# One core, two transformer layers in fp32 accuracy: the start of the recurrent stage in another order

## Chip, cores and metric

One NeuronCore of a Trainium2 chip runs the whole program in one launch. The metric is the device time in microseconds; three runs of the kernel before give a median of 2408.09 us. Its engines are called PE (matrix products; PEld is its weight load), DVE (vector), ACT (scalar), POOL (GpSimd) and SP (which here issues the DMAs).

## What is computed

Two layers on a sequence of 1024 tokens, width 1024. The first has a mixer with four branches (short convolution, stick-breaking attention, a recurrence, spatial gating), gated and merged, and a gated FFN with a short convolution; the second is an attention layer. The change lies in the recurrent branch alone. Per head (4 heads of 64) the reference is

```python
z = z + (token_shift(z) - z) * mu
...
def step(s, inp):
    r_t, w_t, k_t, v_t, a_t, b_t = inp
    sa = jnp.einsum('bhvk,bhk->bhv', s, a_t)
    s = s * w_t[:, :, None, :] + sa[..., None] * b_t[:, :, None, :] + v_t[..., None] * k_t[:, :, None, :]
    return s, jnp.einsum('bhvk,bhk->bhv', s, r_t)
```

The kernel turns the 1024 steps into 16 chunks of 64. Inside a chunk the coupling of the steps is a triangular 64x64 matrix, whose inverse is built by doubling the block size five times (five rounds); the chunks are then chained through their end states.

## The kernel before, in words

**Staging.** All projections are dense products of 128 output channels by 1024 tokens. fp32 accuracy comes from a split: POOL casts a weight block (`w_hi`, L982) and subtracts (`w_lo`, L984), and PE makes three products of it (L1276 to L1278). Block t is split by `split_weights(t)`, which waits until PE has finished block t-2, since two blocks share the buffers. Blocks 24 to 31 (`T_RW` to `T_BR` - 1) feed the recurrence; block 32 (`T_BR`) is the first of the output weights of the branches and is used only after the recurrence's rounds.

**PSUM.** There are 8 banks: `sm` is banks 0 to 3, `gp` banks 4 to 7 (slot 0 is banks 4 and 5, slot 1 banks 6 and 7). The eight dense blocks use the two slots in turn, so the last of them, block 31, ends in banks 6 and 7. ACT scales each result into `zr` (L2327), then DVE adds the shifted one, reading the same banks (`rk_shift(i)`, L2891); the semaphore `p_free0` or `p_free1` says that the slot is free.

**Preparation (DVE).** Channels come in two tiles of 128, ft = 0 and 1. After the shifts, `prep_kk`, `prep_decay`, `prep_keys` and `prep_ends` make the factors `rk_a`, `rk_b`, `rk_e`, `rk_f` and the bonus `rk_vb` of a tile. The last multiplication of `prep_keys` (L2936) makes `rk_f`. `prep_ends` multiplies the bonus (L2940, signal `rk_vb`), adds a bias to it (L2943), makes `rk_e` (L2944) and signals `rk_prep` (L2945). The order of the calls is written out by hand: ..., `prep_keys(1)`, `rk_shift(6)`, `prep_ends(1)`, `rk_shift(7)`, then the matrices.

**Matrices.** `rk_products(ft, o, lhs, rhs)` on PE (L1590) makes 64x64 products of all chunks and both heads of a tile into the bank pair o, o+1. `rk_mats_m` makes b·a into banks 2 and 3 and a·b into banks 6 and 7, `rk_mats_rest` three more: b·q into banks 0 and 1, k·q into 2 and 3, k·a into 4 and 5. DVE's `rk_mats_m` masks them: `m_t` (L2977) and `inv_t` (L2978) from banks 2 and 3, `inv` (L2980) from banks 6 and 7, then adds the identity to `inv` and `inv_t` (L2982, signals `rk_mats_taken` 1 and 2). DVE's `rk_mats_rest` (L2988) masks the other three (`rk_mats_taken` 3 to 5). PE's second pair waits for `p_free1`, that is for `rk_shift(7)`, since it writes into the banks that the shift reads.

**Rounds.** `rk_rounds(ft, beside)` has five rounds. PE multiplies the level matrix `m_lv`, which POOL makes (L1107, `rk_levels`), with `inv` (L1678), ACT copies the result (`m_p`, L2392), PE makes the next two products (L1690, L1693), and DVE adds them to `inv` and `inv_t` (L3004, L3005). Between the two halves of a round PE turns one of eight factors into token order (`rk_turn(n)`, L1626), always into banks 6 and 7. ACT copies the even turns out, DVE the odd ones: `tokens_1` (L3015), called after DVE's additions of a round; `rk_turn(n)` waits for the copy of turn n-1. So `rk_turn(2)` stands behind `tokens_1(0)`. Turns 4 to 7 belong to the second tile and read its `rk_a`, `rk_e`, `rk_f`.

After the second tile's rounds come the chain over the chunks and the merging of the branches, in which PE waits for `w_split` of block 32 for the first time.

Of the kernel before, what the change touches and what calls it, by code (L numbers as in the profile page):

```python
# [35 lines left out]
ALU = mybir.AluOpType  # L36
# [158 lines left out]
def hybrid_layers(nc, x, mix_norm_g, w_in, gate_b, sc_conv_w, sc_out, sb_out, rw_mu, rw_w0, rw_w2,  # L195
# [10 lines left out]
    with ExitStack() as ctx:  # L206
# [740 lines left out]
        def _(pool):  # L947
# [133 lines left out]
            for t in range(T_RW + 1, T_BR + 1):  # L1081
                split_weights(t)
# [29 lines left out]
            rk_levels(0)  # L1112
            pool.wait_ge(s["rk_tok_t"], 7)
# [148 lines left out]
        def _(pe):  # L1262
# [331 lines left out]
            def rk_mats_m(ft):  # L1594

                pe.wait_ge(s["rk_prep"], ft + 1)
                rk_products(ft, 2, rk_b[ft], rk_a[ft])
                if ft == 0:
                    pe.wait_ge(s["p_free1"], frees_before(P_BR))
                else:  # L1600
                    pe.wait_ge(s["rk_tok1"], 4)
                rk_products(ft, 6, rk_a[ft], rk_b[ft])

            def rk_mats_rest(ft):

                k_t, q_t = zr[:, 2 + ft, :], zr[:, ft, :]
                rk_products(ft, 0, rk_b[ft], q_t)
                pe.wait_ge(s["rk_mats_taken"], 5 * ft + 1)
                rk_products(ft, 2, k_t, q_t)
                if ft == 0:  # L1610
                    pe.wait_ge(s["p_free0"], frees_before(P_BR))
                else:
                    pe.wait_ge(s["rk_x_added"], 10)
                rk_products(ft, 4, k_t, rk_a[ft])

            def rk_turn(n):

                ft, kind = divmod(n, 4)
                if n == 0:
                    pe.wait_ge(s["rk_mats_taken"], 2)  # L1620
                else:
                    pe.wait_ge(s[f"rk_tok{(n - 1) % 2}"], (n - 1) // 2 + 1)
# [1075 lines left out]
        def _(dve):  # L2698
# [219 lines left out]

            def prep_keys(ft):
# [16 lines left out]
                wait.after(dve.tensor_tensor(chunks(f), chunks(zk), ends(ft), ALU.mult))  # L2936

            def prep_ends(ft):
                dve.wait_ge(s["rk_bonus_p"], ft + 1)
                dve.tensor_tensor(rk_vb[ft], sm[:, 2:4, :].rearrange("p a b -> p (a b)"), zr[:, 4 + ft, :], ALU.mult) \  # L2940
                    .then_inc(s["rk_vb"], 1)
                dve.wait_ge(s["rk_vb"], ft + 1)
                dve.tensor_scalar(rk_vb[ft], rk_vb[ft], pcol("gn_b", ft), None, ALU.add)  # L2943
# [18 lines left out]
            rk_shift(7)  # L2962
# [11 lines left out]
            def rk_mats_m(ft):  # L2974
# [5 lines left out]
                wait.after(dve.tensor_tensor(flat(inv), four(6), mask(9), ALU.mult))  # L2980
# [3 lines left out]
            def rk_mats_rest(ft):  # L2984
                n = 5 * ft
                for k, (dst, b, m) in enumerate(((rb_t, 0, 2), (rk_t, 2, 2), (n_t, 4, 1))):
# [30 lines left out]

            def post_xa(ft, n):
# [25 lines left out]
            rk_mats_m(0)  # L3044
            rk_mats_rest(0)
            rk_rounds(0, tokens_1)
# [465 lines left out]
```

## Time and profile before

| | us |
|---|---|
| runs: median (lowest to highest) | 2408.09 (2404.7 to 2410.54) |
| the profiled execution: its time | 2407.09 |
| its span in the trace | 2405.4 |
| PE busy in the span | 2349.3 (98%) |
| DVE, ACT, POOL busy | 1186.8, 784.9, 1129.6 |

Positions in the trace are microseconds from the span's start. In a row of the timeline the columns are start, duration, engine, line, operation, output<-inputs with sizes, count, and in brackets the idle time of the engine before it and who ended it. Rows of small instructions of one line are merged; xN is their count. A DVE instruction's successor can start about 0.1 us before its end, so the distance of two starts is less than the duration.

### The profile page before, as it was taken

Reading aid. Unit: us, or ns where it says so; the run is one execution under the profiler, and the core shown is the slowest. Engines: PE = TensorE matmul, PEld = TensorE weight load, DVE = VectorE, ACT = ScalarE, POOL = GpSimd, SP = SyncE. Lnnn points to the kernel's source line nnn. Section 1 sums busy time; section 2 is a strip of 40 time slices with the busy share of each in tenths; the row PEclk is TensorE's granted clock in tenths of the full one; section 3 lists DMA queues with packets and bytes.
Section 4 is the critical chain, followed back from the end, with each engine's and each line's share of the span. In section 5 each row is a group of like instructions: output and inputs, shape, how many; then the busy total and the mean of one; then the engine's idle time right before and its main releaser. Section 6 shows DMA issues by size and latency. Waiting matters only on the chain.

```text
span 2405.4 us, 36383 instructions
## 1 busy us (share of the span) xinstructions
PE 2349.3 (98%) x15466; PEld 1872.4 (78%) x15466; DVE 1186.8 (49%) x1460; ACT 784.9 (33%) x1217; POOL 1129.6 (47%) x771
## 2 busy tenths in 40 slices
PE   7999999999999999999999999999999999999999
PEld 6888888667778868878888887888778886666777
DVE  7811111564285364676666675333455217756621
ACT  4233331433322121254444442110433006565511
POOL 5477762333234278577777773433742220013221
PEclk9999999999999999999999999999999999999999
DMA  5233322101200056423222235222213112001024
GB/s 202 80 105 106 105 99 59 36 27 53 62 19 30 21 182 186 140 72 94 81 88 79 79 97 192 88 105 69 51 38 114 46 43 62 15 10 27 2 69 124
DMA packets 208251, 189.83 MB, mean 79 GB/s; under 512 B 16714, under 2 KB 186929, under 8 KB 207834
## 3 DMA queue, kind: packets, MB, share of 16 engines
q1 hardware_dynamic: 208090, 187.51, 24.8%
q8 instruction: 123, 2.02, 0.4%
q14 instruction: 38, 0.31, 0.0%
HBM read 141.31 MB, written 45.13 MB: 78 GB/s over the span
## 4 chain that ended last, share of the span: by engine, by line
PE 89%; DVE 6%; ACT 2%; POOL 1%; issue 1%; DMA 1%; SPq 0%; DVEq 0%; POOLq 0%; ACTq 0%
PE gp L1276 8%; PE gp L1278 8%; PE gp L1277 8%; PE sm L1839 3%; PE sm L1837 3%; PE sm L1838 3%; PE gp L1837 3%; PE gp L1839 3%; PE gp L1838 3%; PE gp L1965 3%; PE gp L1981 2%; PE gp L1422 2%; PE gp L1424 2%; PE gp L1423 2%; PE sm L1454 2%; PE gp L1454 2%
## 5 line engine op out<-in xcount | busy, mean ns | idle before, releaser
L982 POOL CAST w_hi<-w_raw 128x1024 fp32r<-128x1024 f32 (+1 forms) x97 | 107.5, 1108 | 688.3 <-PE gp L1278 317.4
L984 POOL TENSOR_TENSOR w_lo<-w_raw,w_hi 128x1024 fp32r<-128x1024 f32 (+1 forms) x105 | 284.4, 2709 | 8.3 <-ACT w_hi L2407 0.5
L1276 PE MATMUL gp<-h_hi,w_hi 128*128 128x512 f32 x656 | 260.6, 397 | 0.0
L1278 PE MATMUL gp<-h_hi,w_lo 128*128 128x512 f32 x656 | 255.5, 389 | 0.0
L1277 PE MATMUL gp<-h_lo,w_hi 128*128 128x512 f32 x656 | 255.3, 389 | 0.0
L1276 PEld LDWEIGHTS gp<-h_hi,w_hi 128*128 128x128 f32 x656 | 123.2, 188 | 29.9 <-issue 4.9
L1277 PEld LDWEIGHTS gp<-h_lo,w_hi 128*128 128x128 f32 x656 | 123.2, 188 | 27.3 <-issue 2.4
L1278 PEld LDWEIGHTS gp<-h_hi,w_lo 128*128 128x128 f32 x656 | 123.1, 188 | 25.9
L1192 POOL TENSOR_TENSOR w_lo<-w_sum,w_hi 128x512 fp32r<-128x512 f32 x66 | 96.3, 1459 | 45.7 <-ACT w_hi L2466 45.7
L2874 DVE TENSOR_TENSOR_SCAN sb_run<-sb_keep,ones_row 128x128 f32<-128x128 f32 (+7 forms) x32 | 74.1, 2355 | 84.9 <-POOL sb_keep L1030 84.9
L2631 ACT ACTIVATE att_s<-att_s,small 128x1024 f32<-128x1024 f32 (+7 forms) x128 | 98.8, 774 | 8.8 <-DVE small L3357 8.5
L1422 PE MATMUL gp<-h_hi,w_hi 128*128 128x512 f32 x208 | 86.1, 414 | 0.0
L1424 PE MATMUL gp<-h_hi,w_lo 128*128 128x512 f32 x208 | 81.6, 392 | 0.0
L2643 ACT COPY att_pt<-gp 128x512 f32<-128x512 f32 (+1 forms) x80 | 44.9, 561 | 111.2 <-PE gp L1965 110.9
L1423 PE MATMUL gp<-h_lo,w_hi 128*128 128x512 f32 x208 | 81.1, 390 | 0.0
L1965 PE MATMUL gp<-ident,att_s 128*128 128x128 f32 x576 | 77.3, 279 | 0.9 <-DVE small L3357 0.9
L2549 ACT CAST g_hi<-g_stage 128x1024 fp32r<-128x1024 f32 x22 | 23.0, 1051 | 166.2 <-DMA g_stage<-g_spill 121.3
L1837 PE MATMUL gp<-x_hi_T,w_hi 128*128 128x512 f32 x176 | 69.8, 396 | 5.9 <-DVE up_u L3195 5.2
L1142 POOL TENSOR_TENSOR merged<-merged,gated 128x1024 f32<-128x1024 f32 x24 | 64.9, 2703 | 18.1 <-DVE gated L3067 15.4
L1965 PEld LDWEIGHTS gp<-ident,att_s 128*128 128x128 f32 x576 | 61.5, 141 | 13.5 <-issue 9.3
L1861 PE MATMUL gp<-g_hi,w_hi 128*128 128x512 f32 x176 | 68.7, 390 | 2.1 <-POOL w_lo L984 1.9
L2466 ACT CAST w_hi<-w_sum 128x512 fp32r<-128x512 f32 x66 | 41.0, 621 | 90.9 <-PE gp L1839 43.6
(661 smaller groups left out, 6421.3 us busy)
## 6 DMA issues: line engine op xcount, KB each, us to landing
w_raw<-in_w_in SPq DMA_DIRECT2D x67, 512.0 KB, 4.0
gate_in<-gates_spill SPq DMA_DIRECT2D x30, 512.0 KB, 4.3
gates_spill<-gate_out SPq DMA_DIRECT2D x28, 512.0 KB, 5.9
w_raw<-in_w_up SPq DMA_DIRECT2D x22, 512.0 KB, 4.9
up_raw<-in_w_up SPq DMA_DIRECT2D x22, 512.0 KB, 5.1
g_spill<-hid SPq DMA_DIRECT2D x22, 512.0 KB, 2.6
g_stage<-g_spill SPq DMA_DIRECT2D x22, 512.0 KB, 4.4
w_raw<-in_w_down SPq DMA_DIRECT2D x22, 512.0 KB, 3.6
```

The source lines that it names most:

```text
L982: pool.tensor_copy(w_hi[:, t % 2, 0:n], w_raw[:, t % 2, 0:n]).then_inc(s["w_high"], 1)
L984: pool.tensor_tensor(w_lo[:, t % 2, 0:n], w_raw[:, t % 2, 0:n], w_hi[:, t % 2, 0:n].bitcast(F32), ALU.subtract).then_inc(s["w_split"], 1)
L1276: pe.matmul(o, wh, hi[:, k0 + k, c], start=(k == 0), stop=False)
L1277: pe.matmul(o, wh, lo[:, low[k] if low else k0 + k, c], start=False, stop=False)
L1278: mm = pe.matmul(o, wl, hi[:, k0 + k, c], start=False, stop=(k == n - 1))
L1422: pe.matmul(o, wh, h_hi[:, k, c], start=(k == 0), stop=False)
L1423: pe.matmul(o, wh, h_lo[:, k, c], start=False, stop=False)
L1424: mm = pe.matmul(o, wl, h_hi[:, k, c], start=False, stop=(k == KT - 1))
L1837: pe.matmul(o, wh, xh[:, :], start=(i < 4 and j == 0), stop=False, skip_group_check=True)
L1838: pe.matmul(o, wh, xl[:, :], start=False, stop=False, skip_group_check=True)
L1839: mm = pe.matmul(o, wl, xh[:, :], start=False, stop=(j == 3), skip_group_check=True)
L1965: mm = pe.transpose(bank(4 + r % 3)[:, P * n:P * n + P], s_buf[:, at_place(u), hh, P * k:P * k + P], ident[:, :])
```

## The change

Four edits. On PE and DVE the second product of the first tile (a·b) goes into banks 0 and 1 in place of 6 and 7, without a wait for `p_free1`, and b·q of the first tile goes into banks 6 and 7 behind that wait; the second tile keeps its banks. On DVE `rk_shift(7)` moves from ahead of the first tile's five mask operations to behind them. On DVE the second tile's `rk_f` multiplication and the rest of its `prep_ends` (bias, `rk_e`, signal `rk_prep`) become `late_ends(1)`, which runs in the first round of the first tile, after its additions and ahead of `tokens_1(0)`; in the first tile the order stays. On POOL `split_weights(T_BR)` moves from ahead of `rk_levels(0)` to behind it.

```diff
--- before.py
+++ after.py
@@ -1078,7 +1078,7 @@
                     for m, c in sb_pieces(step)[2]:
                         if c == sb_parts(m) - 1:
                             sb_cut(m)
-            for t in range(T_RW + 1, T_BR + 1):
+            for t in range(T_RW + 1, T_BR):
                 split_weights(t)
 
             def split_branch(n, y):
@@ -1110,6 +1110,7 @@
                                        ALU.mult).then_inc(s["rk_lv"], 1)
 
             rk_levels(0)
+            split_weights(T_BR)
             pool.wait_ge(s["rk_tok_t"], 7)
             for ft in range(2):
                 ends = small[:, 32 + 16 * ft:48 + 16 * ft].rearrange("p (u q) -> p q u", q=2)
@@ -1595,16 +1596,16 @@
 
                 pe.wait_ge(s["rk_prep"], ft + 1)
                 rk_products(ft, 2, rk_b[ft], rk_a[ft])
+                if ft:
+                    pe.wait_ge(s["rk_tok1"], 4)
+                rk_products(ft, 6 if ft else 0, rk_a[ft], rk_b[ft])
+
+            def rk_mats_rest(ft):
+
+                k_t, q_t = zr[:, 2 + ft, :], zr[:, ft, :]
                 if ft == 0:
                     pe.wait_ge(s["p_free1"], frees_before(P_BR))
-                else:
-                    pe.wait_ge(s["rk_tok1"], 4)
-                rk_products(ft, 6, rk_a[ft], rk_b[ft])
-
-            def rk_mats_rest(ft):
-
-                k_t, q_t = zr[:, 2 + ft, :], zr[:, ft, :]
-                rk_products(ft, 0, rk_b[ft], q_t)
+                rk_products(ft, 0 if ft else 6, rk_b[ft], q_t)
                 pe.wait_ge(s["rk_mats_taken"], 5 * ft + 1)
                 rk_products(ft, 2, k_t, q_t)
                 if ft == 0:
@@ -1617,7 +1618,7 @@
 
                 ft, kind = divmod(n, 4)
                 if n == 0:
-                    pe.wait_ge(s["rk_mats_taken"], 2)
+                    pe.wait_ge(s["rk_mats_taken"], 3)
                 else:
                     pe.wait_ge(s[f"rk_tok{(n - 1) % 2}"], (n - 1) // 2 + 1)
                 pe.wait_ge(s["rk_prep"], ft + 1)
@@ -2916,6 +2917,9 @@
                 zk = zr[:, 2 + ft, :]
                 wait.after(dve.tensor_tensor(zk, zk, rk_b[ft][:, :], ALU.mult))
 
+            def key_ends(ft):
+                wait.after(dve.tensor_tensor(chunks(rk_f[ft][:, :]), chunks(zr[:, 2 + ft, :]), ends(ft), ALU.mult))
+
             def prep_keys(ft):
                 zk, zq, e, f = zr[:, 2 + ft, :], zr[:, ft, :], rk_e[ft][:, :], rk_f[ft][:, :]
                 a, b = rk_a[ft][:, :], rk_b[ft][:, :]
@@ -2933,13 +2937,20 @@
                 dve.scalar_tensor_tensor(a, rk_kk[:, :], -1.0, rk_lx[:, :], ALU.mult, ALU.mult)
                 dve.tensor_tensor(zq, zq, rk_l[:, :], ALU.mult)
                 wait.after(dve.tensor_copy(decay_end(ft), rk_l[:, C - 1:T:C]))
-                wait.after(dve.tensor_tensor(chunks(f), chunks(zk), ends(ft), ALU.mult))
+                if ft == 0:
+                    key_ends(0)
 
             def prep_ends(ft):
                 dve.wait_ge(s["rk_bonus_p"], ft + 1)
                 dve.tensor_tensor(rk_vb[ft], sm[:, 2:4, :].rearrange("p a b -> p (a b)"), zr[:, 4 + ft, :], ALU.mult) \
                     .then_inc(s["rk_vb"], 1)
+                if ft == 0:
+                    late_ends(0)
+
+            def late_ends(ft):
                 dve.wait_ge(s["rk_vb"], ft + 1)
+                if ft:
+                    key_ends(ft)
                 dve.tensor_scalar(rk_vb[ft], rk_vb[ft], pcol("gn_b", ft), None, ALU.add)
                 wait.after(dve.tensor_tensor(chunks(rk_e[ft][:, :]), chunks(rk_b[ft][:, :]), ends(ft), ALU.mult))
                 dve.tensor_copy(small[:, 80:81], ones[:, 0:1]).then_inc(s["rk_prep"], 1)
@@ -2959,7 +2970,6 @@
             prep_keys(1)
             rk_shift(6)
             prep_ends(1)
-            rk_shift(7)
 
             def flat(x):
                 return x[:, :, :, :].rearrange("p h u c -> p (h u) c")
@@ -2977,13 +2987,13 @@
                 dve.tensor_tensor(flat(m_t), four(2), mask(1), ALU.mult).then_inc(s["rk_m"], 1)
                 dve.tensor_tensor(flat(inv_t[ft]), four(2), mask(3), ALU.mult)
                 dve.wait_ge(s["rk_mats"], n + 2)
-                wait.after(dve.tensor_tensor(flat(inv), four(6), mask(9), ALU.mult))
+                wait.after(dve.tensor_tensor(flat(inv), four(6 if ft else 0), mask(9), ALU.mult))
                 for x in (inv, inv_t[ft]):
                     dve.tensor_tensor(flat(x), flat(x), mask(0), ALU.add).then_inc(s["rk_mats_taken"], 1)
 
             def rk_mats_rest(ft):
                 n = 5 * ft
-                for k, (dst, b, m) in enumerate(((rb_t, 0, 2), (rk_t, 2, 2), (n_t, 4, 1))):
+                for k, (dst, b, m) in enumerate(((rb_t, 0 if ft else 6, 2), (rk_t, 2, 2), (n_t, 4, 1))):
                     dve.wait_ge(s["rk_mats"], n + 3 + k)
                     dve.tensor_tensor(flat(dst[ft]), four(b), mask(m), ALU.mult).then_inc(s["rk_mats_taken"], 1)
 
@@ -3015,6 +3025,12 @@
                 dve.tensor_copy((a_tok, b_tok, k_tok, v_tok)[kind][ft][:, :, :],
                                 gp[:, 1, :].rearrange("p (u c) -> p u c", u=NB)).then_inc(s["rk_tok1"], 1)
 
+            def beside_0(n):
+
+                if n == 0:
+                    late_ends(1)
+                tokens_1(n)
+
             def post_xa(ft, n):
                 dve.wait_ge(s["rk_post"], n)
                 dve.tensor_copy(flat(xa[ft]), chunks(gp[:, 1, :])).then_inc(s["rk_post1"], 1)
@@ -3042,8 +3058,9 @@
 
             dve.wait_ge(s["masks"], 1)
             rk_mats_m(0)
+            rk_shift(7)
             rk_mats_rest(0)
-            rk_rounds(0, tokens_1)
+            rk_rounds(0, beside_0)
             rk_mats_rest(1)
             rk_rounds(1, post_1)
             post_xa(1, 7)
```

## Rows read from the trace of the kernel before

**Rows 1.** The page: part 1, first engines, and part 4, the chain by engine.
```profile
PE 2349.3 (98%) x15466; PEld 1872.4 (78%) x15466; DVE 1186.8 (49%) x1460; ACT 784.9 (33%) x1217; POOL 1129.6 (47%) x771
...
PE 89%; DVE 6%; ACT 2%; POOL 1%; issue 1%; DMA 1%; SPq 0%; DVEq 0%; POOLq 0%; ACTq 0%
```

**Rows 2.** Timeline, 690 to 730 us: DVE's preparation and masks, ACT's last dense block.
```profile
700.41 1.23 DVE L2936 TENSOR_TENSOR rk_f<-zr,small 128x1024 f32<-128x1024 f32 x1
...
704.25 0.76 DVE L2943 TENSOR_SCALAR rk_lx<-rk_lx,col 128x1024 f32<-128x1024 f32 x1
...
704.63 1.12 ACT L2327 ACTIVATE zr<-gp,small 128x1024 f32<-128x1024 f32 x1 [12.87 <-PE gp L1278]
...
706.24 1.27 DVE L2891 SCALAR_TENSOR_TENSOR zr<-gp,col,zr 128x1023 f32<-128x1023 f32 x1
...
707.55 1.22 DVE L2977 TENSOR_TENSOR m_t<-sm,masks 128x1024 f32<-128x1024 f32 x1
...
711.07 1.23 DVE L2982 TENSOR_TENSOR inv<-inv,masks 128x1024 f32<-128x1024 f32 x1
...
712.21 1.22 DVE L2982 TENSOR_TENSOR inv_t<-inv_t,masks 128x1024 f32<-128x1024 f32 x1
...
713.35 1.22 DVE L2988 TENSOR_TENSOR rb_t<-sm,masks 128x1024 f32<-128x1024 f32 x1
```

**Rows 3.** The same timeline: PE's five matrix products and the first round.
```profile
704.53 1.16 PE L1590 MATMUL sm<-rk_a,rk_b 64*64 64x64 f32 x64
...
707.57 1.16 PE L1590 MATMUL gp<-rk_b,rk_a 64*64 64x64 f32 x64 [1.88 <-DVE zr L2891]
...
708.55 1.11 PE L1590 MATMUL sm<-zr,rk_b 64*64 64x64 f32 x64
...
712.35 1.72 PE L1590 MATMUL sm<-zr 64*64 64x64 f32 x64 [2.69 <-DVE inv L2982]
...
713.82 1.95 PE L1590 MATMUL gp<-rk_a,zr 64*64 64x64 f32 x64
...
715.53 2.33 PE L1678 MATMUL sm<-inv,m_lv 64*64 64x64 f32 x64
```

**Rows 4.** Busy time by window: window, length, engines, granted clock, DMA share, GB/s.
```profile
712.30:713.80 1.50, 1.45 (x64) 1.45 (x68) 1.50 (x2) 0.00 (x0) 0.00 (x0) 0.64 0.00 0
...
713.80:715.50 1.70, 1.70 (x76) 1.70 (x70) 1.70 (x2) 0.00 (x0) 0.00 (x0) 0.50 0.05 10
...
715.50:717.80 2.30, 2.30 (x77) 2.23 (x69) 1.42 (x2) 0.59 (x1) 0.80 (x1) 0.86 0.00 0
...
717.80:719.00 1.20, 1.20 (x16) 1.03 (x16) 0.00 (x0) 0.67 (x2) 1.20 (x1) 1.00 0.07 14
```

**Rows 5.** Timeline, 722 to 732 us: second round of the first tile.
```profile
723.71 2.08 PE L1678 MATMUL sm<-inv,m_lv 64*64 64x64 f32 x64
...
724.01 1.22 DVE L3015 COPY b_tok<-gp 128x1024 f32<-128x1024 f32 x1
...
725.72 1.09 PE L1626 MATMUL gp<-ident,rk_f 128*128 128x128 f32 x8
...
725.88 2.37 POOL L1107 TENSOR_TENSOR m_lv<-m_t,masks 128x1024 f32<-128x1024 f32 x1 [4.20 <-PE sm L1678]
```

**Rows 6.** Timeline, 690 to 698 us: DVE and POOL beside each other.
```profile
690.75 1.72 POOL L982 CAST w_hi<-w_raw 128x1024 fp32r<-128x1024 f32 x1 [8.25 <-PE gp L1278]
...
691.49 2.06 DVE L2928 TENSOR_TENSOR rk_b<-rk_kk,rk_a 128x1024 f32<-128x1024 f32 x1
...
692.55 3.25 POOL L984 TENSOR_TENSOR w_lo<-w_raw,w_hi 128x1024 fp32r<-128x1024 f32 x1
...
693.58 3.30 DVE L2931 TENSOR_TENSOR rk_b<-rk_b,rk_f 128x1024 f32<-128x1024 f32 x1
```

**Rows 7.** Timeline of POOL, 690 to 800 us.
```profile
708.85 2.36 POOL L1107 TENSOR_TENSOR m_lv<-m_t,masks 128x1024 f32<-128x1024 f32 x1 [13.05 <-DVE m_t L2977]
...
742.77 4.07 POOL L1117 TENSOR_TENSOR s_step<-masks,small 128x512 f32<-128x512 f32 x4 [6.59 <-PE gp L1626]
```

## Prediction

> **What bounds the kernel now.** I read the page first: PE is busy for 98% of the span and holds 89% of the chain that ended last [rows 1]. So a change of order can only give back time in which PE stands idle or slow, and can cost any time in which it makes PE stand idle. I then read the timeline where the diff works, 690 to 730 us, engine by engine. PE runs its last dense block without a gap and makes the first 64x64 product at 704.53 [rows 3]. Then it stops twice: 1.88 us until the last shift on DVE is done, and 2.69 us until DVE has masked `inv` [rows 3]. DVE in the same stretch never stops: `rk_f` at 700.41, bias at 704.25, last shift at 706.24, `m_t` at 707.55, and the five mask operations to 713.35 [rows 2]. So here the chain is DVE's, and after 712.35 it is PE's again. Third, the granted clock by window: after the second stop it is 0.64 and then 0.50 of full, that is 1.2 GHz in place of 2.4, and it is back at 1.00 by 717.8 [rows 4]. From 717.8 on the first tile's rounds are bound by PE, with DVE waiting.
>
> **Working: up to the first round.** The start of PE's first product stays at 704.53, since PE is full until then. It ends at 705.69 [rows 3], and DVE, now free, starts `m_t` at about 705.8 in place of 707.55: 1.75 us won. `inv` reads banks 0 and 1, whose product PE makes at once, one product of 0.98 us later (708.55 less 707.57 [rows 3]), well before DVE asks. The five operations take 713.35 - 707.55 = 5.80 us [rows 2], to 711.60. Only then comes the last shift, 1.27 us [rows 2], to 712.87. Its other input, ACT's scaling, is done at 705.75 [rows 2] and holds nothing. PE's b·q product waits for this shift, and k·q and k·a stand behind it in PE's order. PE answered 0.06 us after the shift in the kernel before (707.57 against 707.51 [rows 2, 3]), so it restarts at 712.93, against 712.35 before: the shift and the addition to `inv_t` now stand ahead of it and eat the 1.75 us. And it then owes three products before the rounds, where it owed two.
>
> The two took 3.18 us (712.35 to 715.53). At 1.2 GHz one costs 715.53 - 713.82 = 1.71 us, at 2.4 GHz 0.98 us [rows 3, 4]. PE will have stood still from about 706.7 to 712.93, 6.2 us, longer than the stop after which the clock fell here, so I take a fall. With two products slow and one fast I get 4.40 us, and the rounds start at 717.33 in place of 715.53. The first round's product then runs at full clock, 2.08 in place of 2.33 us [rows 3, 5], which returns 0.25. Sum: **+1.55 us**. Bounds: all three fast gives 715.87 and +0.1; all three slow, and the next one too, gives 718.06 and +2.5.
>
> **Working: the first round.** `late_ends(1)` holds the `rk_f` multiplication, 1.23 us, and bias, `rk_e` and signal, 706.24 - 704.25 = 1.99 us [rows 2]: 3.2 us. Queued behind it on DVE is `tokens_1(0)`, which started at 724.01 and lasts 1.22 us [rows 5]; behind that copy waits `rk_turn(2)` on PE, since the turns share one pair of banks, and behind the turn all the rest of PE's second round. On the old time scale the copy would run from 727.2 to 728.45, and PE would turn at 728.5 in place of 725.72 [rows 5]: **+2.8 us**. DVE's idle time in a round does not cover this, because the work stands ahead of the copy.
>
> It can be more. POOL makes a level matrix at 725.88 for 2.37 us [rows 5], reading two SBUF operands. In the new order `rk_e`, a DVE multiplication of SBUF operands, would be asked for at about 724.01 + 1.23 + 0.76 = 726.0, less up to 0.1 for the overlap of successive DVE instructions [rows 2, 5], just behind POOL's request, while the bias operation still runs. What such a meeting costs is to be seen in rows 6: POOL's cast ends at 692.47, and the DVE multiplication asked for at 691.49 ends at 693.55, 1.08 us after it; the subtraction ends at 695.80, and the multiplication asked for at 693.58 ends at 696.88, again 1.08 us after it. So DVE waits out the whole POOL instruction. Here POOL would run from about 726.0 to 728.4, `rk_e` end at 729.45, the copy at 730.65, and PE turn at 730.7: +5.0 us in place of +2.8. Ends: 2.8 and 5.0. I take **+5.0**, because in rows 6 the one who asked first went first each time.
>
> A row can be held against this: `inv`'s addition at 711.07 took 1.23 us beside a level matrix that ran from 708.85 to 711.21 [rows 2, 7]. Only 0.14 us of them overlap, so it decides little. The Trainium skill (SBUF — State Buffer, section "SBUF: two separate sides") calls the pair an exclusive lock, which a vector operation with two SBUF inputs and a GpSimd operation that reads SBUF take from each other for a whole instruction; by it this term would be 5.0, by the bare durations 2.8.
>
> **Working: the clock again.** PE would stand from about 725.8 to 730.7, 4.9 us. Before, the clock fell after a stop of 2.69 us and the slow stretch cost 0.49 + 0.73 + 0.25 = 1.5 us against full-clock durations [rows 3, 5]. Ends: 0 and 1.5, as the clock stayed up after the stop of 1.88 [rows 3] and fell after the longer one. The stop ahead is nearer to the longer: **+1.5**.
>
> **What costs nothing.** The split of block 32 leaves 690.75 to 695.80. DVE gets back 2.06 + 3.30 less twice 1.22, 2.9 us [rows 2, 6], and with the 3.2 us of late ends is ready long before 704.5; but PE is full until then, so this wins nothing beyond the 1.75 already counted. Should that cover be gone, it would be worth up to that much again. The split's new place is POOL's idle time before 742.77, 6.59 us [rows 7]; even at the durations with DVE in the way, 1.72 + 3.25 [rows 6], it fits. Without that gap the diagonal steps would be late, which nobody asks for until the second tile's rounds. DVE's work there reads PSUM. SP's next weight load waits for this split, but stands behind a wait for a product of the second tile's rounds. ACT's sigmoid of the gate input and its table load wait for the last shift and move to about 713 to 715.5, ahead of its first copy of the round. The second tile's `rk_prep` is needed only at turn 4.
>
> **Sum.** 1.55 + 5.0 + 1.5 = 8.05, say +8.1 us. Behind the stage PE's work is the same and shifts whole. Against the profiled execution (span 2405.4, time 2407.09) this is 2415.2; the median of the runs is 1.0 above that execution, so I forecast **2416.2**. A measurement of this kernel tells some 0.2%, 4.8 us, from no change.
>
> **Rivals.**
> - *POOL comes second.* `rk_e` gets ahead of the level matrix, less than 0.1 us decides [rows 5]. 1.55 + 2.8 is +4.4, with the clock's second fall +5.9: 2412.5 to 2414.0. For it: the margin. Against it: rows 6.
> - *Not slower.* The clock stays at 2.4 GHz through both stops. Then the first part costs 0.1 only, and with POOL second the whole is 0.1 + 2.8 = +2.9: 2411.0, inside 0.2%. Place: PE's restarts at 712.9 and in the second round; it decides if both windows show 1.00. For it: the stop of 1.88 us left the clock up. Against it: both new stops are longer than 2.69.
> - *Worse.* Clock down for all three products and once more as long in the second round: 2.5 + 5.0 + 3.0 = +10.5, 2418.6.
> - *Faster.* The turn does not feel the late ends, or the first shift and mask order turns out shorter than I add up: then 1.75 us of earlier `m_t` and 1.5 us of a fall that goes away are the most there is, 2404.8 to 2408. The code speaks against it, since the wait for the copy is written out.
>
> **Chances.** Forecast 0.45, POOL second 0.25, not slower 0.14, worse 0.10, faster 0.06. POOL second lies on both sides of 4.8 us, half and half. So slower 0.68, within 0.2% 0.26, faster 0.06. The range goes from 2410 (one us under the not-slower case, for the measurement) to 2419 (the worse case): it leaves out the faster case and little of the others.
>
> **What would show it.** In the profile after: `m_t` near 705.8; the last shift near 711.6; PE idle some 6 us, ended by L2891, with a granted clock of 0.5 behind it; the first L1678 near 717.3; in the second round L1626 with an idle time of 2.7 (POOL second) or 4.9 us (POOL first), ended by L3015, and `rk_e` at 1.2 or near 3.4 us. I am wrong if the first L1678 comes at 715.5 or sooner, if L1626 has no such idle time, or if something behind 860 us takes the shift up.

## The result, and the profile after

| | kernel before | changed kernel |
|---|---|---|
| median (lowest to highest), us | 2409.32 (2404.7 to 2410.7) | 2419.57 (2417.55 to 2421.22) |
| ratio, 95% interval | | 1.0047 (1.0035 to 1.0059) |
| span of the profiled execution | 2405.4 | 2416.3 |
| mean granted clock of PE in it | 0.996 | 0.992 |

The changed kernel is slower: the medians differ by 10.3 us, and the ratio of 1.0047 is worth some 11 us. The forecast was 2416.2 with a range from 2410 to 2419: the sign was right, the size too small, and the median lies 0.6 us outside the range. In two later sets of runs the changed kernel gave 1.0046 (1.0033 to 1.0059) and 1.0039 (1.0025 to 1.0053). All ratios here are of fast runs; one run of the kernel "banks sooner, b·q sooner" took 13344.08 us and is in none of them.

The page of the changed kernel, parts 1 and 4, against [rows 1]: PE's busy time is up by 4.8 us, and the span by 10.9.

```profile
PE 2354.1 (97%) x15466; PEld 1877.7 (78%) x15466; DVE 1185.9 (49%) x1460; ACT 784.8 (32%) x1217; POOL 1127.3 (47%) x771
...
PE 89%; DVE 5%; ACT 2%; POOL 2%; issue 1%; DMA 1%; SPq 0%; DVEq 0%; POOLq 0%; ACTq 0%
```

PE's timeline, against [rows 3, 5] (line numbers behind L1590 are one higher):

```profile
704.22 1.16 PE L1591 MATMUL sm<-rk_a,rk_b 64*64 64x64 f32 x64
...
705.21 1.11 PE L1591 MATMUL sm<-rk_b,rk_a 64*64 64x64 f32 x64
...
712.65 1.99 PE L1591 MATMUL gp<-zr,rk_b 64*64 64x64 f32 x64 [6.33 <-DVE zr L2892]
...
714.41 1.74 PE L1591 MATMUL sm<-zr 64*64 64x64 f32 x64
...
715.98 1.10 PE L1591 MATMUL gp<-rk_a,zr 64*64 64x64 f32 x64
...
716.92 2.04 PE L1679 MATMUL sm<-inv,m_lv 64*64 64x64 f32 x64
...
723.79 1.09 PE L1627 MATMUL gp<-ident,rk_e 128*128 128x128 f32 x8
...
731.78 1.97 PE L1627 MATMUL gp<-ident,rk_f 128*128 128x128 f32 x8 [4.89 <-DVE b_tok L3025]
...
738.72 1.10 PE L1627 MATMUL gp<-ident,zr 128*128 128x128 f32 x8
```

The two stops that the change makes stand in the brackets: 6.33 us for the last shift, 4.89 us for the token copy. The kernel before had 1.88 and 2.69 us there, and no stop in the second round. The last row is the fourth turn; from the third to the fourth it took 6.94 us, where the kernel before took 4.91 (725.72 to 730.63 in its trace).

DVE's timeline, and the POOL row beside it:

```profile
705.52 1.22 DVE L2987 TENSOR_TENSOR m_t<-sm,masks 128x1024 f32<-128x1024 f32 x1 [5.79 <-PE sm L1591]
...
711.32 1.27 DVE L2892 SCALAR_TENSOR_TENSOR zr<-gp,col,zr 128x1023 f32<-128x1023 f32 x1
...
725.11 1.22 DVE L2921 TENSOR_TENSOR rk_f<-zr,small 128x1024 f32<-128x1024 f32 x1
...
726.36 0.75 DVE L2954 TENSOR_SCALAR rk_lx<-rk_lx,col 128x1024 f32<-128x1024 f32 x1
...
727.03 3.38 DVE L2955 TENSOR_TENSOR rk_e<-rk_b,small 128x1024 f32<-128x1024 f32 x1
...
730.51 1.22 DVE L3025 COPY b_tok<-gp 128x1024 f32<-128x1024 f32 x1
...
726.98 2.34 POOL L1107 TENSOR_TENSOR m_lv<-m_t,masks 128x1024 f32<-128x1024 f32 x1 [4.19 <-PE sm L1679]
```

`m_t` starts at 705.52 (forecast 705.8), the shift at 711.32 (711.6). `rk_e` takes 3.38 us: POOL's level matrix is asked for at 726.98, `rk_e` at 727.03. 726.98 + 2.34 + 1.08 = 730.40, the end of `rk_e`. This is the meeting of [rows 6] once more.

Busy time and granted clock by window (columns as in [rows 4]):

```profile
706.40:709.00 2.60, 0.00 (x0) 0.00 (x0) 2.60 (x3) 0.35 (x1) 2.17 (x1) 1.00 0.02 6
...
709.00:712.60 3.60, 0.00 (x0) 0.00 (x0) 3.56 (x4) 0.00 (x0) 0.18 (x1) 0.50 0.00 0
...
712.60:714.40 1.80, 1.75 (x64) 1.75 (x68) 0.00 (x0) 1.75 (x2) 0.00 (x0) 0.50 0.00 0
...
714.40:716.90 2.50, 2.50 (x140) 2.50 (x134) 1.89 (x2) 0.59 (x1) 0.00 (x0) 0.72 0.02 7
...
716.90:718.90 2.00, 2.00 (x81) 1.93 (x69) 1.69 (x2) 0.59 (x1) 0.79 (x1) 1.00 0.00 0
...
731.70:735.20 3.50, 3.42 (x36) 3.09 (x38) 0.02 (x1) 1.01 (x1) 0.00 (x0) 0.50 0.00 0
...
735.20:738.70 3.50, 3.50 (x106) 3.45 (x102) 1.28 (x2) 0.00 (x0) 0.00 (x0) 0.84 0.02 5
...
738.70:742.00 3.30, 3.30 (x78) 3.04 (x75) 2.42 (x3) 0.71 (x2) 0.07 (x1) 1.00 0.02 5
```

In the profiled execution of the kernel before, the clock fell 0.4 us after PE had restarted and stayed down for 3.4 us, all of it work at 1.2 GHz. Here it falls inside the stop: from 709.0 on it is 0.50, while PE does nothing, and the mixed window of 0.72 puts its return at 715.8, so it was down for 6.8 us. The second fall runs from 729.5, within the second stop, to 736.3: 6.8 us again.

### The profile page after: what moved, and what is told of

It is laid out like the page before. It is cut to its first block, busy times and chain, and to the rows that moved or that the text cites. A ratio compares the mean times of both kernels' runs of the same rounds, so it can differ in the third digit from the quotient of the medians.

```text
span 2416.3 us, 36384 instructions
## 1 busy us (share of the span) xinstructions
PE 2354.1 (97%) x15466; PEld 1877.7 (78%) x15466; DVE 1185.9 (49%) x1460; ACT 784.8 (32%) x1217; POOL 1127.3 (47%) x771
## 4 chain that ended last, share of the span: by engine, by line
PE 89%; DVE 5%; ACT 2%; POOL 2%; issue 1%; DMA 1%; SPq 0%; DVEq 0%; POOLq 0%; ACTq 0%
PE gp L1277 8%; PE gp L1279 8%; PE gp L1278 8%; PE sm L1839 3%; PE sm L1838 3%; PE sm L1840 3%; PE gp L1838 3%; PE gp L1839 3%; PE gp L1966 3%; PE gp L1840 3%; PE gp L1982 2%; PE gp L1423 2%; PE gp L1425 2%; PE gp L1424 2%; PE sm L1456 2%; PE gp L1456 2%
## 5 line engine op out<-in xcount | busy, mean ns | idle before, releaser
L1143 POOL TENSOR_TENSOR merged<-merged,gated 128x1024 f32<-128x1024 f32 x24 | 64.8, 2700 | 19.9 <-DVE gated L3084 17.2
```

## The experiments

All times of marks below are microseconds from PE's first 64x64 product (the one at 704.22 here), since the stretch ahead of it varies by up to 1.7 us between executions. "First round" is the start of the first product of `inv` and the level matrix (L1678 before), a "turn" the start of `rk_turn` of that place (L1626 before). The marks are of one execution each. The ratios are to the kernel before, with 95% intervals.

| kernel | first round | second turn | third turn | fourth turn | ratio |
|---|---|---|---|---|---|
| before | 11.0 | 18.2 | 21.2 | 26.1 | |
| before, again | 11.0 | 17.9 | 20.9 | 25.8 | 0.9995 (0.9986 to 1.0004) |
| changed | 12.7 | 19.6 | 27.6 | 34.5 | 1.0047 (1.0035 to 1.0059) |
| changed, again | 13.6 | 20.5 | 28.5 | 36.0 | 1.0046 (1.0033 to 1.0059) |
| changed, third time | 13.6 | 20.9 | 28.8 | 36.5 | 1.0039 (1.0025 to 1.0053) |
| copy ahead of the late ends | 13.6 | 20.6 | 23.6 | 28.5 | 1.0013 (1.0004 to 1.0021) |
| ends back in the preparation | 12.7 | 19.6 | 22.6 | 27.5 | 1.0014 (1.0005 to 1.0023) |
| level matrix waits | 13.6 | 20.6 | 26.4 | 32.9 | 1.0026 (1.0015 to 1.0036) |
| idle products, many | 14.0 | 22.2 | 32.8 | 37.7 | 1.0049 (1.0036 to 1.0062) |
| idle products, fewer | 12.7 | 19.9 | 27.9 | 32.8 | 1.0033 (1.0021 to 1.0045) |
| shift ahead again | 10.5 | 17.4 | 25.4 | 32.7 | 1.0031 (1.0021 to 1.0041) |
| before + split moved | 10.6 | 17.4 | 20.5 | 25.4 | 1.0003 (0.9994 to 1.0012) |
| before + split + free banks | 10.8 | 17.6 | 20.7 | 25.6 | 0.9996 (0.9988 to 1.0005) |
| before + late ends | 10.3 | 17.7 | 25.7 | 33.4 | 1.0034 (1.0022 to 1.0047) |
| banks sooner | 10.8 | 19.2 | 22.3 | 27.2 | 1.0013 (1.0004 to 1.0023) |
| banks sooner, b·q sooner | 9.6 | 17.0 | 20.1 | 25.0 | 1.0007 (0.9998 to 1.0016) |
| the same, first tile alone | 8.5 | 16.3 | 19.3 | 24.2 | 0.9999 (0.9991 to 1.0007) |

### What the late ends cost

**The copy first.** In the changed kernel:

```diff
-                if n == 0:
-                    late_ends(1)
                 tokens_1(n)
+                if n == 0:
+                    late_ends(1)
```

> The changed kernel with the first token copy (L3025) ahead of late_ends(1) in the first round; nothing else differs. Theory A (the copy behind the late ends is what stops PE): PE's third turn has no stop of 4.9 us before it, the clock stays up in the second round, and the time falls by 5.0 + 2.0 = 7 us, to about 2412.5. Late ends then last until some 731, so DVE's additions of the second round may come up to 1 us late. Theory B (the stop has another cause, or the loss lies behind the stage): the stop or the time stays, within 2 us of 2419.6.

The third turn comes 3.0 us behind the second, as before the change, and the ratio falls from 1.0047 to 1.0013, some 8 us. DVE's timeline:

```profile
725.43 1.22 DVE L3025 COPY b_tok<-gp 128x1024 f32<-128x1024 f32 x1
...
727.81 2.74 DVE L2954 TENSOR_SCALAR rk_lx<-rk_lx,col 128x1024 f32<-128x1024 f32 x1
...
731.81 0.69 DVE L3014 TENSOR_TENSOR inv<-inv,sm 128x512 f32<-128x512 f32 x1
```

Now the bias operation meets POOL and takes 2.74 us, and the additions of the second round start as soon as the late ends are through, about 1.5 us late. This costs PE some 0.4 us behind the fourth turn (3.4 us to the fifth in place of 3.0). Theory A holds.

**The ends back in the preparation**, ahead of the matrices, with the other three edits kept:

```diff
-                if ft == 0:
-                    key_ends(0)
+                key_ends(ft)
...
-                if ft == 0:
-                    late_ends(0)
+                late_ends(ft)
```

> The changed kernel with the second tile's ends back in prep_ends(1) and prep_keys(1), before the matrices; bank pair, last shift and weight split stay as changed. Theory A: as with the copy first, 7 us less than the changed kernel, about 2412.5, with m_t still at 705.5 because the split's new place has made room for the ends; what is left over the kernel before (2409.3) is the first part, 1.4 us, and clock falls elsewhere. Theory B (the ends were worth moving, because DVE was late for the first masks): m_t goes back towards 707.5 and the gain is 2 us smaller.

`m_t` starts 1.3 us after the first product, as in the changed kernel, and DVE had stood idle for 2.39 us ahead of it: the ends were not in the way once the split had moved. Fourth turn at 27.5, time +3.4 us. Theory B falls.

**No POOL beside the late ends.** POOL's fourth level matrix waits for them:

```diff
                         pool.wait_ge(s["rk_p"], 2 * (z - 2))
+                        if z == 4:
+                            pool.wait_ge(s["rk_prep"], 2)
```

> The changed kernel in which POOL's fourth level matrix of the first tile waits until the late ends are signalled (rk_prep 2), so that no POOL instruction runs beside them. Theory A (rk_e waits out the POOL instruction): rk_e takes 1.22 us in place of 3.38, the stop before the third turn is 2.7 us in place of 4.9, the time falls by 2.2 us, and by up to 2 more if the clock then stays up: 2415.4 to 2417.4. Theory B (rk_e is long for a reason of its own): it stays at 3.4 us and the time at 2419.6.

DVE's row of `rk_e` and PE's row of the third turn:

```profile
727.74 1.22 DVE L2957 TENSOR_TENSOR rk_e<-rk_b,small 128x1024 f32<-128x1024 f32 x1
...
730.33 1.09 PE L1629 MATMUL gp<-ident,rk_f 128*128 128x128 f32 x8 [2.73 <-DVE b_tok L3027]
```

1.22 us in place of 3.38, and a stop of 2.73 us in place of 4.89: the 2.2 us are the POOL instruction that `rk_e` waited out. Behind the shorter stop the clock was down for 3.4 us in place of 6.8, and from third to fourth turn it took 6.45 us. The ratio falls to 1.0026, some 5 us less than the first ratio of the changed kernel (2.2 to 4.2 were expected), and the fourth turn is 1.6 to 3.6 us sooner; the intervals of the ratios overlap, so only the direction and the rows are shown.

**The late ends alone**, on the kernel before (`key_ends`, `late_ends` and `beside_0` of the change, nothing else):

```diff
-            rk_rounds(0, tokens_1)
+            rk_rounds(0, beside_0)
```

> The kernel before with one edit: the second tile's ends in the first round, ahead of the token copy. The last shift then is no longer behind the ends but, with the split where it was, DVE has 3.2 us less to do before it. Theory A: the first part wins 0.7 us (the shift waits for ACT and ends at 706.8), the third turn comes 5 us later and the clock's fall costs 2 more: some 6.3 to 7 us over the kernel before. Theory B (the stop is seen only together with the other edits): under 3 us.

The stop is 4.89 us here too, the fourth turn comes at 33.4, 7.5 us later than before, and the ratio is 1.0034, +8.2 us, where 6.3 to 7 was expected. This one edit carries most of the loss.

### What the shift's new place costs

In the changed kernel, `rk_shift(7)` ahead of the masks again:

```diff
             prep_ends(1)
+            rk_shift(7)
...
             rk_mats_m(0)
-            rk_shift(7)
```

> The changed kernel with rk_shift(7) back ahead of the first masks; free bank pair, late ends in the first round and weight split stay as changed. Theory A (the shift behind the masks is what costs the first part): b·q no longer waits, PE owes two products behind the inverse's mask as before, and since DVE is early the shift is done at 706.8, m_t starts at 706.8 and the rounds at some 714.7 in place of 716.9: 2.2 us less than the changed kernel, some 9 us over the kernel before. Theory B (m_t's earlier start is worth its price): moving the shift ahead costs 1.3 us.

PE's rows of b·q, k·q and the first round:

```profile
705.77 1.16 PE L1591 MATMUL gp<-zr,rk_b 64*64 64x64 f32 x64 [0.50 <-DVE zr L2892]
...
710.55 1.99 PE L1591 MATMUL sm<-zr 64*64 64x64 f32 x64 [3.62 <-DVE inv L2993]
...
713.71 2.04 PE L1679 MATMUL sm<-inv,m_lv 64*64 64x64 f32 x64
```

b·q is out of the way 1.6 us after the products ahead of it, and the first round starts at 10.5 in place of 12.7 or 13.6. Measured: 1.0031, below the changed kernel's 1.0047, 1.0046 and 1.0039, but with an interval that overlaps all three; the marks of the first round (2.2 to 3.1 us sooner) carry Theory A, and the size of the gain in time is left open.

A sharper pair stands in the table: "ends back in the preparation" and "before + split + free banks" differ in the place of this shift alone. With the shift behind the masks the second turn comes 2.0 us later (19.6 against 17.6), the fourth 2.0 us later (27.5 against 25.6), and the ratios are 1.0014 and 0.9996, from two sets of runs. This is the price of the shift's new place, without the late ends.

**Split moved alone**, and **split moved with the free bank pair**, both on the kernel before:

```diff
-            for t in range(T_RW + 1, T_BR + 1):
+            for t in range(T_RW + 1, T_BR):
                 split_weights(t)
...
             rk_levels(0)
+            split_weights(T_BR)
```

> The kernel before with one edit: the split of block 32 behind rk_levels(0). Theory A: DVE's preparation gets 2.9 us back, the last shift then waits for ACT and is done at 706.8 in place of 707.5, so the stage ends 0.7 us sooner: 0 to 1 us under the kernel before. Theory B (the split's new place delays POOL's later work): level matrices or s_step come later than before and the time rises.

> The kernel before with the split moved and the inverse's product in banks 0 and 1, but last shift and second tile's ends where they were. Theory A (the free bank pair by itself wins nothing, since behind the earlier shift the old banks are free as soon as DVE asks): within 1 us of the kernel with the split moved alone. Theory B (the free pair is a gain by itself): the rounds start earlier than with the split alone.

The marks stand at 10.6 and 10.8 for the first round, 0.2 to 0.4 us sooner than before, and at 25.4 and 25.6 for the fourth turn. The ratios hold 1. The split's new place is free and the free pair wins nothing: DVE is early, waits 2.38 us for ACT's scaling, and the shift behind it frees the old banks in time.

### What the clock costs

Idle products on PE in both stops, into banks that are overwritten later (`fill(n)` is n groups of 32 matrix products like L1590's, which the trace counts as 64; five groups ahead of the wait for `p_free1`, four ahead of the third turn):

```diff
                 if ft == 0:
+                    fill(5, True)
                     pe.wait_ge(s["p_free1"], frees_before(P_BR))
...
                 if place < 8:
+                    if place == 2:
+                        fill(4, False)
                     rk_turn(place)
```

> The changed kernel with idle work on PE: five more 64x64 product groups (some 4.9 us) into the free banks 4 and 5 in the wait for the last shift, and four more (some 3.9 us) ahead of the third turn; their results are overwritten. If the clock's fall behind the two stops costs time of its own, the granted clock stays at 1.00 in both places, the three products take 2.9 us in place of 4.3, the second round 4.9 in place of 6.9, and the time falls by 3.4 us to about 2416. If the falls cost nothing of their own, the time stays at 2419.6 or rises.

```profile
705.98 2.16 PE L1603 MATMUL gp<-rk_a,rk_b 64*64 64x64 f32 x135
...
709.31 2.09 PE L1603 MATMUL gp<-rk_a,rk_b 64*64 64x64 f32 x128 [1.17 <-issue]
...
712.77 1.05 PE L1603 MATMUL gp<-rk_a,rk_b 64*64 64x64 f32 x57 [1.36 <-issue]
...
729.24 7.68 PE L1603 MATMUL gp<-rk_a,rk_b 64*64 64x64 f32 x256
...
736.85 1.09 PE L1639 MATMUL gp<-ident,rk_f 128*128 128x128 f32 x8
```

The fillers ran over: the first five ended at 713.6, with 1.17 and 1.36 us in which PE waited for nothing but its own issue, and the second four took 7.68 us in place of 3.9. So the time says nothing of the clock's price, but the clock was 1.00 in both places and the third turn was followed by the fourth after 4.90 us, not 6.94. With fewer:

```diff
-                    fill(5, True)
+                    fill(3, True)
...
-                        fill(4, False)
+                        fill(2, False)
```

> As the kernel with idle products on PE, whose fillers ran over the two stops (they ended at 713.6 and 736.9), with fewer of them: three groups in the first stop, two in the second. Theory A (the clock's fall has a price of its own, 1.5 to 2 us each): the clock stays at 1.00 or falls later and shorter, the second round takes 4.9 to 6 us from turn to turn in place of 6.9, and the time is 2 to 3.5 us under the changed kernel's. Theory B: the fillers only add their own time, and the time is that of the changed kernel or more.

Busy time and clock by window, fillers and what follows, first and second stop:

```profile
706.40:710.80 4.40, 3.23 (x210) 3.00 (x200) 4.37 (x5) 0.68 (x1) 2.38 (x1) 1.00 0.02 4
...
713.00:716.30 3.30, 3.30 (x128) 3.30 (x132) 1.18 (x1) 2.31 (x2) 0.00 (x0) 0.52 0.02 5
...
727.30:731.30 4.00, 4.00 (x136) 3.88 (x132) 3.97 (x4) 0.59 (x1) 2.37 (x1) 1.00 0.01 4
...
732.40:737.30 4.90, 4.86 (x136) 4.67 (x136) 1.29 (x2) 1.01 (x1) 0.00 (x0) 1.00 0.01 3
```

At the first stop the clock still fell, in the 2.15 us that were left. At the second it stayed at 1.00, with 1.13 us of stop left and the copy no earlier than before (third turn at 27.9), and from third to fourth turn it is 4.90 us again. The fourth turn comes at 32.8 in place of 34.5 to 36.5; the ratio, 1.0033, lies below the changed kernel's 1.0039 to 1.0047, but its interval overlaps theirs. What shows the price is the row: with the copy as late as before and the same work behind it, but the clock up, third to fourth turn takes 4.90 us in place of 6.94 to 7.64. So the fall of the clock has a price of its own, 2.0 to 2.7 us in this place.

### The changed kernel and the kernel before, again

> The changed kernel itself, once more, beside its variants. The stage, from PE's first product to the fourth turn, took 34.5 us against 26.1 before, +8.4; the whole was measured at +11.3 us (8.4 to 14.2). Theory A (nothing behind the stage is slower for a reason of its own; the clock falls there come by chance of an execution): +8.5 to +9.5 us here. Theory B (the stage's delay makes something behind it slower): +11 or more again.

> The kernel before itself. Its stage was seen in one execution only (26.1 us from PE's first product to the fourth turn, with one fall of the clock), and two executions of the changed kernel took 34.5 and 36.0. If the clock's falls set the stage's spread in both kernels, this execution lies between 25.5 and 27.5, and the part behind the fourth turn between 1672 and 1679 us, as in all kernels so far. The ratio of times is 1.000 within its interval.

> The changed kernel a third time. The stage takes 34 to 36.5 us, the part behind the fourth turn 1672 to 1679 us. If the whole is again 11 us over the kernel before while stage and end part explain 8.4 to 9.9, the rest is how often the clock falls behind the stage; if it is 9 to 10, nothing is left open.

The kernel before gives 25.8 beside 26.1; the changed kernel 36.0 and 36.5 beside 34.5. Windows of the third execution of the changed kernel:

```profile
709.00:713.00 4.00, 0.00 (x0) 0.00 (x0) 3.97 (x4) 0.00 (x0) 0.59 (x1) 0.50 0.00 0
...
714.80:716.50 1.70, 1.70 (x76) 1.70 (x72) 1.23 (x1) 0.60 (x1) 0.00 (x0) 0.50 0.00 0
...
716.50:718.20 1.70, 1.70 (x76) 1.70 (x70) 1.23 (x1) 0.00 (x0) 0.00 (x0) 0.50 0.04 10
...
737.00:741.10 4.10, 4.10 (x104) 4.04 (x100) 1.28 (x2) 0.00 (x0) 0.00 (x0) 0.69 0.01 4
```

The first row is the stop, the next two are the second and third product: here all three products and part of the first round ran at 1.2 GHz (1.70 us each), while in the first execution the third product was fast again. From third to fourth turn the second and third executions took 7.46 and 7.64 us.

How long the clock stays down goes with the stop ahead of it; the lengths are read from windows like these, set ever closer around a fall. In the stage it was down for 3.4 us at every stop of 2.15 to 3.62 us (both executions of the kernel before among them) and for 6.8 us at every stop of 4.89 us. At the stops of 6.33 and 6.34 us it was 6.8 us, and 10.2 us once, in this third execution. The part from the fourth turn to the end of the span was 1677.6, 1674.8 and 1677.2 us for the changed kernel, 1674.8 and 1674.9 for the kernel before, and 1672.5 to 1678.7 over all kernels here. Most of that spread is the clock too. In the first execution of the changed kernel it fell four times behind the stage, in the kernel before twice (the last two rows):

```profile
876.30:879.60 3.30, 3.30 (x9) 2.17 (x7) 0.00 (x0) 0.00 (x0) 3.30 (x2) 0.50 0.67 226
...
1057.20:1063.90 6.70, 6.10 (x14) 4.85 (x15) 4.63 (x6) 4.38 (x7) 4.84 (x5) 0.50 0.00 0
...
1490.70:1494.00 3.30, 3.30 (x9) 2.54 (x9) 3.30 (x4) 1.04 (x1) 3.22 (x2) 0.50 0.70 209
...
2006.10:2009.40 3.30, 3.30 (x16) 2.89 (x16) 2.73 (x8) 3.01 (x6) 0.00 (x0) 0.50 0.00 0
...
1047.30:1054.00 6.70, 5.09 (x12) 4.07 (x13) 5.00 (x7) 4.84 (x8) 4.84 (x4) 0.50 0.00 0
...
2163.40:2166.70 3.30, 3.30 (x16) 1.39 (x13) 0.78 (x4) 0.00 (x0) 3.30 (x2) 0.50 0.22 50
```

Over the 17 traces of this document the part behind the fourth turn is 1672.5 to 1674.8 us where the clock was down for 6.8 us in it, 1674.8 to 1676.9 for 10.2 us (both executions of the kernel before), 1675.3 to 1677.2 for 13.7 us, and 1677.6 to 1678.7 for 17 to 20.5 us. The three executions of the changed kernel have 17.1, 6.8 and 13.7 us. Whether the change makes such falls more frequent, three executions do not tell.

### A better order?

The products k·q and k·a wait for the addition to `inv`, though banks 2 and 3 are free once `m_t` and `inv_t` are masked. On the kernel with the split moved:

```diff
-                dve.tensor_tensor(flat(m_t), four(2), mask(1), ALU.mult).then_inc(s["rk_m"], 1)
                 dve.tensor_tensor(flat(inv_t[ft]), four(2), mask(3), ALU.mult)
+                dve.tensor_tensor(flat(m_t), four(2), mask(1), ALU.mult).then_inc(s["rk_m"], 1)
...
-                pe.wait_ge(s["rk_mats_taken"], 5 * ft + 1)
+                pe.wait_ge(s["rk_m"], ft + 1)
```

> The kernel before with the split moved, and with PE's k·q product waiting for the last read of banks 2 and 3 (the masks of inv_t, then m_t, in this order, signal rk_m) in place of the addition to inv. Theory: PE's stop shrinks from 3.6 us to under 1, the products run while DVE masks, the clock stays up, and the rounds wait for the mask of b·q on DVE, to 713.9 in place of 715.5: 1.5 us and up to 1 more under the kernel before. Rival (DVE's chain sets the start of the rounds anyway): less than 1 us.

```profile
710.82 2.36 DVE L2983 TENSOR_TENSOR inv<-inv,masks 128x1024 f32<-128x1024 f32 x1
...
715.51 3.01 PE L1679 MATMUL sm<-inv,m_lv 64*64 64x64 f32 x64 [2.89 <-DVE rb_t L2989]
```

It is slower than the kernel before. POOL's level matrix, which follows `m_t`, is now late and meets the addition to `inv`, which takes 2.36 us; PE, done early, stands 2.89 us for DVE's b·q mask, and the clock falls in its first round (3.01 us in place of 2.08). The rival was right. Next, in the first tile, b·q's mask ahead of the addition to `inv_t`:

```diff
+                    if ft == 0 and x is not inv:
+                        rk_taken(0, 0)
                     dve.tensor_tensor(flat(x), flat(x), mask(0), ALU.add).then_inc(s["rk_mats_taken"], 1)
...
-                pe.wait_ge(s["rk_mats_taken"], 5 * ft + 3)
+                pe.wait_ge(s["rk_mats_taken"], 8 if ft else 2)
```

> As the kernel with the banks sooner, and in the first tile the mask of b·q goes ahead of the addition to inv_t, with the rounds waiting for that. Theory: the rounds start one DVE operation sooner, at 712.8: another 1.1 us, some 2.5 to 3 us under the kernel before. Rival (inv_t's addition is then late for the second half of the first round): no more than the kernel with the banks sooner.

The fourth turn comes at 25.0, but the ratio is 1.0007 (0.9998 to 1.0016): no gain is shown. Last, `m_t` first again, and the sooner wait in the first tile alone (`inv_t`'s mask counts on `rk_m` too):

```diff
-                dve.tensor_tensor(flat(inv_t[ft]), four(2), mask(3), ALU.mult)
+                ins = dve.tensor_tensor(flat(inv_t[ft]), four(2), mask(3), ALU.mult)
+                if ft == 0:
+                    ins.then_inc(s["rk_m"], 1)
...
+                    pe.wait_ge(s["rk_m"], 2)
```

> The kernel with b·q sooner, mended: m_t again goes first, so that POOL's level matrix is done before inv's addition (which took 2.35 us beside it, in place of 1.22), and PE's wait is shortened in the first tile alone. Theory: the rounds start 8.3 us after PE's first product in place of 11.0, and if the clock stays up the fourth turn comes 23.6 us after it in place of 26.1: 2 to 3 us under the kernel before. Rival: PE's stop before the rounds makes the clock fall in the first round and the gain is under 1 us.

PE's rows of k·q, the first round and the fourth turn:

```profile
709.17 1.16 PE L1591 MATMUL sm<-zr 64*64 64x64 f32 x64 [0.29 <-DVE inv_t L2982]
...
712.72 2.08 PE L1682 MATMUL sm<-inv,m_lv 64*64 64x64 f32 x64 [0.43 <-DVE rb_t L2995]
...
728.38 1.09 PE L1630 MATMUL gp<-ident,zr 128*128 128x128 f32 x8
```

The first round starts at 8.5 in place of 11.0 and the fourth turn comes at 24.2, 1.9 us sooner than before. The ratio is 0.9999 (0.9991 to 1.0007), which allows that gain and none. In the profiled executions of the last two kernels the clock did not fall in the stage at all, but it was down for 20.5 us behind the fourth turn, and that part took 1678.7 us where the kernel before took 1674.8: more than the stage had won. Whether the one brings the other is not shown. No version here is shown to beat the kernel before; several equal it and beat the changed kernel.

## Why the prediction was right in kind and too small

- **First product to first masks:** right. `m_t` 1.3 us after the product, as forecast; the preparation had 5.79 us to spare.
- **The shift behind the masks, three products owed:** right in mechanism (stop 6.33 us, forecast 6.2), too small in size. The step that failed is "with two products slow and one fast": at the second turn the three executions stand 1.5, 2.5 and 2.8 us behind the kernel before (19.6, 20.5, 20.9 less the mean of 18.2 and 17.9), where the sum had 1.55. In the profiled execution the sum fitted; in the two others all three products were slow. The slow stretch of [rows 4] was taken as the measure, and there the clock was down for 3.4 us. Behind the longer stop it was down for 6.8 us, and 10.2 us in the third execution.
- **The late ends ahead of the copy, with POOL going first:** right. From second to third turn it is 8.0 us in all three executions and 3.0 before: +5.0, forecast +5.0. The rival "POOL comes second" did not occur in the changed kernel; POOL's wait shows what it would have given.
- **The second fall of the clock:** the other step that failed. Forecast 1.5, measured 2.0, 2.6 and 2.7 (6.94, 7.46, 7.64 less 4.90). The price came from one stretch behind a stop of 2.69 us, in which PE worked at half clock for 3.4 us. Behind a stop of 4.89 us the clock was down for 6.8 us in each of the three executions, and PE worked through 4.5 us of it in the first one (731.78 to 736.3). With the shorter stop of "level matrix waits" it was 3.4 us and a cost of 1.55 us, near the forecast.
- **Sum:** 1.5 to 2.8, 5.0, 2.0 to 2.7 give 8.5, 10.0 and 10.5 us where 8.05 was forecast.
- **Behind the stage:** "PE's work is the same and shifts whole" put this term at nothing. In the profiled execution it was the larger part of the miss: of its 10.9 us the stage has 8.4 (forecast 8.05) and the part behind it 2.8, with the clock down for 17.1 us there in place of 10.2. Over the three executions that part is 1676.5 us on average against 1674.9. These 1.6 us lie within the spread of all kernels, so that they belong to the change is not shown.
- **The range:** "worse", both falls longer, was priced at +10.5 us, 2418.6, and given 0.10. Two of the three executions came near it (+10.0 and +10.5 in the stage; the first part of the third, 2.8, even passed the bound of 2.5). The range ended 0.4 us above it, with no room for the measurement: the kernel before itself gave medians of 2406.1 to 2409.3 in five sets, and 1.2 us of the distance to the forecast is that its median was 2409.32 beside the changed kernel and 2408.09 when the forecast was made.
- **What costs nothing:** right for the split and the bank pair, each shown by a run. I did not see that the ends' move was needless too: with the split moved, DVE idles 2.39 us ahead of the first masks even with the ends in place.
- **The rival "not slower"** needed a clock that stays up through stops of 6.3 and 4.9 us. In three executions it never did. The Trainium skill (TensorE: Matmul & The Clock Gate, Part 1) says of this gate that "K is binary": half of the pulses pass or all of them; a third ratio that it names needs three or more busy cores on a die, and this kernel, on one core, can show nothing of it. The windows agree, with 0.50 and 1.00 wherever a window is not mixed.

## What to carry over

Work that is moved into an engine's idle time belongs behind what the next engine waits for: DVE had 3.65 us of idle time in a round of the kernel before, and 3.2 us of late ends ahead of a 1.2 us copy still stopped PE for 4.9. When a change lengthens a stop of PE, price the stop and then the slow clock behind it, and remember that it grows with the stop: here the clock was down twice as long behind 4.89 us as behind 2.69. Take the price from the longest stop that the trace has, with the whole of the work that follows counted at half clock as the upper end. Ask first which of several edits makes room: here one of them, the split, had already freed all that the others were meant to free.

## What was not expected

- Stops of 1.13 us and, in the kernel before, 1.88 us left the clock up; one of 2.15 us did not, though more than 3 us of idle products ran ahead of it. No run here has a stop between 1.88 and 2.15 us in the stage, and whether the length of the stop alone decides is not shown.
- The same 64 small products take 0.98 us where four tile positions follow each other (L1590) and 1.92 us where two neighbours in the order use the same position (the second filler, 7.68 us for 256). The two fillers differ in nothing else but this, and that the second uses two of the four positions.
- Idle products were held up by PE's own issue, for 1.17 us in both fillers and again for 1.36 us in the longer one, so idle work is not free even where PE stands still. Such holds came without fillers too, 0.59 to 0.80 us inside k·a, in the three kernels in which PE no longer waits for the addition to `inv`.
- Over 23 executions of the kernel before, those with a mean clock of 0.997 took 2405.2 us on average (4 of them) and those with 0.994 took 2410.0 (2). How much of the spread goes with the clock differs: the correlation of time and mean clock is -0.49 in this set and -0.67, -0.74 and -0.89 in three others.
